# A decoder layer with attention, a state-space branch and 16 experts: three expert halves requested before the last projection job, decay products in bf16 parts, the router's logits in four streams, and two products of resident rows ahead of the ranks

## The reference

```python
sh1, sc1, gt1, sh2, sc2, gt2 = split(silu(c) @ w_mod + b_mod, 6)
h = rms_norm(x, g_norm1) * (1 + sc1) + sh1
q, k, v, fl, z, xbc, dtr, ga, gb = split_cols(h @ w_in)
o_att = forgetting_attention(rms_norm(q), rms_norm(k), v, cumsum(log_sigmoid(fl + b_f)))
u = silu(causal_conv(xbc)); xs, bm, cm = split_cols(u)
dt = softplus(dtr + dt_bias); acs = cumsum(dt * a)          # per chunk of 128 tokens
lmat = exp(acs[t] - acs[s])                                  # for s <= t, per head
y = (cm @ bm.T * lmat) @ (xs * dt) + (cm * exp(acs)) @ state + d_skip * xs
y = group_rms_norm(y * silu(z)) * g_ssm
x = x + gt1 * ((sigmoid(ga) * (o_att @ w_pa) + sigmoid(gb) * (y @ w_pb)) @ w_o)
h2 = rms_norm(x, g_norm2) * (1 + sc2) + sh2
probs = softmax(h2 @ w_router + b_router)    # 16 experts in 4 groups
# group with the largest probability, its two best experts, weights normalised over the two
x = x + gt2 * sum_over_two(w * ((silu(h2 @ w_gate[e]) * (h2 @ w_up[e])) @ w_down[e]))
```

## Time and profile before

| | |
|---|---|
| timed runs | 795.19, 796.26, 804.49 us; median 796.26 |
| profiled execution | 794.72 us, of it span 793.1 us |
| PE / weight loads / DVE / ACT / POOL busy | 757.5 / 523.0 / 366.0 / 296.7 / 94.4 us |
| chain that ended last | PE 75%, DVE 7%, ACT 6%, DMA 5%, issue 4% |
| DMA | 219.5 MB, mean 277 GB/s |
| mean granted clock of PE | 0.989 |

### The profile page before, as it was taken

How to read it: one execution, slowest core, us unless ns; L and a number is a source line. 1 busy time by engine, 2 the same in 40 slices (tenths; PEclk the granted TensorE clock), 3 DMA queues, 4 the chain that set the end, 5 groups by cost and what they waited for, 6 DMA issues and landing times.

```text
span 793.1 us, 12477 instructions
## 1 busy us (share of the span) xinstructions
PE 757.5 (96%) x4545; PEld 523.0 (66%) x4545; DVE 366.0 (46%) x852; ACT 296.7 (37%) x736; POOL 94.4 (12%) x155
## 2 busy tenths in 40 slices
PE   3799999999999999999998999999999999999997
PEld 3376787778785687888877888888444444444444
DVE  1355657777773186587999211022321223122214
ACT  3223257657773224668884001012412112221212
POOL 3321012112101114320100100000010000000000
PEclk9799999999999999999999999999899999999999
DMA  9996365969866512349999694363999999999992
GB/s 319 331 343 190 107 199 156 337 213 330 271 230 205 179 54 60 111 143 376 372 313 363 220 402 156 107 248 128 385 380 420 420 420 420 418 421 418 423 407 73
DMA packets 94040, 219.48 MB, mean 277 GB/s; under 512 B 11765, under 2 KB 67645, under 8 KB 80024
## 3 DMA queue, kind: packets, MB, share of 16 engines
q1 hardware_dynamic: 78928, 181.71, 62.7%
q0 software_dynamic: 7840, 31.67, 11.7%
q10 hardware_dynamic: 7208, 5.25, 2.1%
HBM read 207.05 MB, written 13.22 MB: 278 GB/s over the span
## 4 chain that ended last, share of the span: by engine, by line
PE 75%; DVE 7%; ACT 6%; DMA 5%; issue 4%; SPq 1%; POOLq 1%; ACTq 0%; POOL 0%; DVEq 0%
PE bank L1681 16%; PE bank L2015 14%; PE bank L1911 7%; PE bank L2039 7%; PE bank L1614 4%; PE bank L1919 4%; PE bank L2058 3%; PE bank L1893 3%; DMA conv_out<-in_w_mod 3%; PE bank L1677 2%; PE bank L1635 2%; DMA arena<-in_state_ssm 2%; DVE arena L1417 1%; ACT arena L1031 1%; PE bank L1828 1%
## 5 line engine op out<-in xcount | busy, mean ns | idle before, releaser
L1681 PE MATMUL bank<-h_normed,weight_ring 128*128 128x264 f32 x1024 | 237.2, 388 | 1.7 <-ACT conv_work L1039 1.7
L1681 PEld LDWEIGHTS bank<-h_normed,weight_ring 128*128 128x128 f32 x1024 | 191.4, 190 | 36.9 <-issue 3.5
L2015 PE MATMUL bank<-arena,h_normed 128*64 128x512 f32 x176 | 79.0, 604 | 0.0
L1911 PE MATMUL bank<-y_T,weight_ring 128*128 128x264 f32 x256 | 57.4, 386 | 0.4 <-DVE y_T L1454 0.4
L1541 DVE SCALAR_TENSOR_TENSOR x_residual<-bank,modulation,x_residual 128x256 f32<-128x256 f32 x64 | 28.8, 484 | 55.4 <-PE bank L2058 55.4
L1911 PEld LDWEIGHTS bank<-y_T,weight_ring 128*128 128x128 f32 x256 | 48.5, 190 | 8.7 <-issue 0.5
L1534 DVE TENSOR_TENSOR arena<-arena,bank 128x512 f32<-128x512 f32 x8 | 8.5, 1066 | 98.5 <-PE bank L2015 98.5
L1614 PE MATMUL bank<-identity,arena 128*128 128x128 f32 (+5 forms) x218 | 31.6, 287 | 13.6 <-ACT arena L859 9.6
L1031 ACT ACTIVATE arena<-conv_out,early_small 128x128 f32<-128x128 f32 x128 | 38.3, 388 | 11.3 <-DVE arena L1417 10.7
L2015 PE MATMUL bank<-weight_ring,h_normed 128*64 128x512 f32 x144 | 42.0, 594 | 0.0
L1614 PEld LDWEIGHTS bank<-identity,arena 128*128 128x128 f32 (+5 forms) x218 | 26.4, 152 | 22.5 <-POOL arena L713 9.6
(11 more groups left out here) (374 smaller groups left out, 1208.2 us busy)
## 6 DMA issues: line engine op xcount, KB each, us to landing
weight_ring<-in_w_in SPq DMA_DIRECT2D x36, 1024.0 KB, 6.3
weight_ring<-in_w_mod SPq DMA_DIRECT2D x22, 1024.0 KB, 10.0
arena<-in_w_up SPq DMA_DIRECT2D x12, 1024.0 KB, 20.0
weight_ring<-in_w_down SPq DMA_DIRECT2D x12, 1024.0 KB, 23.3
arena<-in_w_gate SPq DMA_DIRECT2D x10, 1024.0 KB, 17.7
weight_ring<-in_w_gate SPq DMA_DIRECT2D x10, 1024.0 KB, 14.8
arena<-in_state_ssm POOLq DMA_DIRECT2D x8, 1024.0 KB, 10.1
out_ssm_sample<-arena POOLq DMA_DIRECT2D x8, 1024.0 KB, 8.3
```

What stands on the lines that cost most here:

```text
L1681: ins = mm(ps[:, 0:T], w, hT[:, c, :], start=c == 0, stop=c == KD - 1)
L1911: ins = mm(ps[:, 0:T], w, yT[:, c, :], start=c == 0, stop=c == NXB - 1)
L2015: ins = mm(banks[i][BLK * e:BLK * e + BLK, :], xg[:, 4 * h + c, BLK * e:BLK * e + BLK], ws[e][c], start=h == 0 and c == 0, stop=h == 1 and ...
```

## The change

Five edits:

1. Early expert halves. Half 16 goes behind `pb` 7. The ring's slots are filled singly, each when its own last `o` job is done, in the order of these jobs. Ahead of the last ring part SP waits for the merged branches and loads half 15. Half 13 follows behind `o` 7. The last slot in the arena is moved by 128 columns for that.
2. Decay products. The running sums are split in three bf16 parts (rounded value, rounded rest, rest of that), stacked in 96 partitions by DVE and two transfers of ACT; `ab` multiplies them by a 96-row one-hot matrix `head_pick` in bf16. A pair is no longer interleaved over two row strips. The copy to partitions 64 up goes away.
3. The `exp` job goes. The skip vector comes by a fifth transfer on ACT, behind the three scratch stores (four requests), and DVE makes `dsk` from it by two copies behind a wait for all of them. The bank rotation is turned by one from `bt` on, so that all later jobs keep their banks.
4. Logits. `lg` is done for two blocks at a time, as four products of 264 columns on four column strips of 32: two for the logits of the two blocks (weights padded to 32 columns), two for the squares' sums. A job `lgt` follows: ACT copies the 264 columns to SBUF, PE folds the strips and turns them to rows by three products with a 0/1 matrix `fold`. Two of the six `hx` jobs go ahead: one ahead of the last `lg`, one ahead of the fold.
5. Ahead of the ranks, two products of 256 columns of `ones` with a block of x into the bank of the ranks, read by nobody. The weights' semaphore is merged in that of the assignment.

Core of the diff:

```diff
-        jobs += [("bs", 0), ("bs", 1), ("exp",)]
+        jobs += [("bs", 0), ("bs", 1)]
...
-            if i:
-                jobs += [("lg", i - 1)]
-        jobs += [("lg", 7)] + [("hx", a, f) for a in range(3) for f in range(2)] + [("rk",)]
+            if i and i % 2 == 0:
+                jobs += [("lg", i // 2 - 1)]
+        jobs += [("lg", 3), ("lgt",)] + [("hx", a, f) for a in range(3) for f in range(2)] + [("rk",)]
...
+        ring_places = sorted(((8 + 4 * (k // 2) + k % 2 + 2 * q, 2 * i + q) for k, i in enumerate(ring_order) for q in range(2)),
+                             key=lambda p: (jobs.index(last_user[held_by[p[1]]]), p[0]))
...
-            for i in ring_order:
-                filled_by(ring_last[i])
-                n = 4 + ring_order.index(i)
-                load_expert(n)
-            filled_by(("o", 7))
-            load_expert(7)
             load_half(16)
+            for m, i in ring_places:
+                if i == ring_places[-1][1]:
+                    sp.wait_ge(m_ready, KD)
+                    load_half(15)
+                filled_by(last_user[held_by[i]])
+                load_half(m)
+            load_half(13)
...
                         act.dma_start(se_d, ex[:]).then_inc(bs_out, 16)
+                        act.dma_start(dskf, t["d_skip"].to_broadcast([128, SH])).then_inc(bs_out, 16)
...
                     if a == 0 and b == 0:
-                        dve.wait_ge(bs_out, 64)
+                        dve.wait_ge(bs_out, 80)
+                        for q in range(2):
+                            r = slice(64 * q, 64 * q + 64)
+                            link(v.tensor_copy(dsk[r, :], dskf[r, q:SH:2]))
...
-                    for i in range(4):
-                        for q in range(2):
-                            h, r = 4 * (b + q) + i, 64 * q
-                            ins = mm(pair[q][:, 128 * i:128 * i + 128],
-                                     ident[r:r + SH, r + h:r + h + 1].to_broadcast([SH, 128]),
-                                     acsT[r:r + SH, 128 * a:128 * a + 128], start=True, stop=True)
+                    for q in range(2):
+                        for i in range(4):
+                            h = 4 * (b + q) + i
+                            ins = mm(pair[q][:, 128 * i:128 * i + 128], head_pick[:, h:h + 1].to_broadcast([3 * SH, 128]),
+                                     acs3[:, 128 * a:128 * a + 128], start=True, stop=True)
+                        done(ins, ("ab", a, b + q))
...
+                    for q in range(2):
+                        mm(sbank[32 * q:32 * q + 32, 0:T], wr32[:, 2 * r + q, :], hT[:, 2 * r + q, :], start=r == 0,
+                           stop=r == 3, tile_position=(0, 32 * q), skip_group_check=True)
+                    for q in range(2):
+                        ins = mm(sbank[64 + 32 * q:96 + 32 * q, 0:T], onesf[:, 0:32], sqr[:, (2 * r + q) % 4, :], start=r == 0,
+                                 stop=r == 3, tile_position=(0, 64 + 32 * q), skip_group_check=True)
...
+                elif k == "lgt":
+                    rows_flipped(("hx", 0, 1))
+                    pe.wait_ge(lgs_ready, 1)
+                    for a, (t0, n) in enumerate(TOK):
+                        ins = mm(logits[0:n, a, 0:NE + 1], lgs[:, t0:t0 + n], fold[:], start=True, stop=True)
+                    ins.then_inc(lgt_done, 1)
...
+                    for _ in range(2):
+                        mm(ps[:, 0:NP], onesf[:], xT[:, 0, 0:NP], start=True, stop=True)
```

More of the change, by code:

```diff
@@ L682, in _ @@
             link(g.memset(cT, 0.0), consts)
+            for p in range(3):
+                r = slice(SH * p, SH * p + SH)
+                link(g.tensor_copy(head_pick[r, :], ident[r, r]))
             link(g.memset(onesf[:], 1.0))
@@ L919, in _ @@
                     link(fn(fdw[0:SH, 2, 0:128], fdw[0:SH, 2, 0:128], ACT.Exp))
-                    link(fn(ex[:, NS:2 * NS], ex[:, NS:2 * NS], ACT.Exp), fd_e)
+                    link(fn(ex[:, NS:2 * NS], ex[:, NS:2 * NS], ACT.Exp), fd_exp)
                 elif k == "ft":
                     read_out(act, j)
+                    act.wait_ge(acs_split, 1)
+                    for p in range(2):
+                        act.dma_start(acs3[SH * (p + 1):SH * (p + 2), :], acs_low[:, NP * p:NP * p + NP])\
+                           .then_inc(acs_stacked, 16)
                     act.dma_start(t["logf_prompt"].rearrange("o b (a p) h -> p (o b a) h", p=128),
```

134 lines of the change are left out of this document (76 added, 58 removed).

## The result

| | before | changed |
|---|---|---|
| timed runs beside each other, 16 each: median (lowest to highest) | 797.05 (795.15 to 804.49) us | 794.29 (788.48 to 799.97) us |
| ratio changed / before | | 0.9943, interval 0.9918 to 0.9969 |
| profiled execution, span | 793.1 us | 798.0 us |
| mean granted clock in it | 0.989 | 0.973 |

The ratio is 4.5 us of gain (2.5 to 6.5). The forecast was a gain of 6.0 by the medians (796.26 to 790.3). The profiled execution of the changed kernel is the slowest of its 16, 4.9 us of span longer than the one of before, so its profile has to be read by stages, and not by its end.

The account below looks back on a forecast made before the run. PE sets the pace, with transfers near their limit in the expert stage. Logits 4.4 plus decay 1.9 minus 0.5 after the last `o` minus 0.4 for the skip vector gives 5.4 us off: timed median 790.3 us, range 785.5 to 796.

Parts of the forecast that it names:

- the prediction's own case: Whole kernel: the summed terms hold, timed median 790.3 us, range 788 to 793, chance 0.56.
- Logits: Between `o` jobs: three groups of four products replace six slots of small products, gain 4.4 us.
- After the last `o`: Last logit group to ranks: square root comes later, some of it regained, net cost 0.5 us (0.2 to 1.2).
- Decay products: `ab` pairs: bf16 products at 0.10 us each, 0.27 less a pair, seven pairs, gain 1.9 us (1.0 to 4.6).
- the rival that spoke of the floor: `ab` pairs: bf16 products near their floor, 0.44 us a pair, another 2.7 us off, 787.6; chance 0.12.
- Skip vector: Ahead of the first decay pair: removed products gain nothing, ACT's extra request costs 0.4 us (0.2 to 0.8).
- The 2 us bring nothing: First decay pair: without the 32 products PE arrives 2 us earlier but only waits for ACT's copies.
- Three halves: Expert weight stream: asking for three halves earlier is worth nothing in itself, since the stream breaks before the first freed half.
- the prediction's own sign of being wrong: Profile after: a clock of 0.5 anywhere in 277 to 285 or through the gather would show the prediction wrong.
- The rival with two more low stretches of 1.8 us on the path: New pauses ahead of first decay pair and ranks lower the clock: gain only 1.8 us, 793.9; chance 0.16.
- The stretch at the gate: First gate products: a rival had the low-clock stretch miss them, 1.8 us more gained, 788.5; chance 0.08.
- the rival that had 0.04: Gather and gate start: all at 1.2 GHz, 7 to 9 us lost, 798.3; chance 0.04.

Follow-up runs that it names:

- u_skip: Changed kernel with edit 3 undone (spreading products back, skip vector's transfer and two copies gone): 793.5 us, ratio 0.9924 to before.
- best: skip_early with the shift products ahead of the ranks replacing the resident products there, and resident products in two other PE waits: 792.24 us, ratio 0.9927 to before.
- best_state: best with eight more resident products in three PE waits of the state stage: 791.15 us, ratio 0.9906 to before.
- dense10: Changed kernel with ten products of resident rows instead of two, spread from the last logit group to the token numbers: 795.04 us, ratio 0.9954 to before.
- again: Changed kernel unaltered, timed and profiled once more: 795.69 us, ratio 0.9937 to before.
- u_decay: Changed kernel with edit 2 undone (float32 decay products on two row strips): 798.81 us, ratio 0.9997 to before.
- u_logits: Changed kernel with edit 4 undone (twelve small products of a block behind each projection job): 798.22 us, ratio 0.9995 to before.
- skip_early: Changed kernel with the skip vector's transfer moved to SP near 28 us and DVE's copies made earlier: 791.79 us, ratio 0.9906 to before.

## Why the forecast was right, and where it was not

The median, 794.29, is in the range of 785.5 to 796, but outside the 788 to 793 that the prediction's own case allowed, and 4.0 above the 790.3 forecast (0.8 of it is that before's median is 797.05 here and not 796.26). That the gain, 4.5 us, came near the 5.4 of the sum is in part luck: the parts are worth 3.1 more than forecast at full clock, and about 4.0 were lost in two ways, one that the sum left to the rivals and one that it didn't have.

**Logits: right.** 4.4 us were forecast, and the stage is 35.59 - 30.98 = 4.6 shorter in every profile that has the edit. The group costs 0.58, not 0.46; what made up for it is that `o` jobs back to back take 3.56 to 3.66, not 3.76.

**After the last `o`: right.** 0.5 forecast, 8.35 - 8.01 = 0.34 found; the square root 1.94 us behind the group where 2.1 stood.

**Decay products: mechanism right, size wrong.** The step that failed is the price of a bf16 product of 128 columns. It was taken as 0.10 us, from a 16-column row and a quarter of float32's price per column; it is 0.61 / 8 = 0.076 in the timeline, 0.55 / 8 = 0.069 in the chain, and 0.45 / 8 = 0.056 in the chain for two of the six pairs that counted. These six, not seven, gained 4.1 us, not 1.9: 0.54 to 0.64 in the pair itself, and 0.14 in the projections right behind four of them, which the prediction did not reckon with. That is nearer the rival that spoke of the floor (7 x 0.65 = 4.6) than the case chosen. The Trainium skill's figure for it, about 81 ns on the page "TensorE: Matmul & The Clock Gate", section "Back-to-back issue gap", would have given 3.1, nearer than the forecast.

**Skip vector: sum nearly right, both reasons wrong.** 0.4 us of cost forecast, 0.62 found (u_skip). "The 2 us bring nothing" was wrong: from the turning to the first pair it took 6.59 us with `exp` and float32, 5.88 now and 5.40 with the request gone too. ACT's copies begin 4.55 us after the turning, one request more ahead of them, where before had 5.12: the store to `sx_scratch` held ACT for 1.42 us before and 0.40 now. In both profiles with `exp` one of these requests was 1.0 us longer than in the twelve without it; why is not shown. The claim that DVE's longer wait for the new vector ends at about the same time as its wait for PE was wrong by 1.9 us, for the vector lands late and the copies meet POOL's multiply.

**Three halves: right.** No effect seen, and the stream breaks as described.

**Low clock: the prediction's own sign of being wrong was seen.** It named a clock of 0.5 through the gather. The rival with two more low stretches of 1.8 us on the path had 0.16 and gives 793.9; that the median is near this is no proof of it. A stretch behind the pause of the first decay pairs is in three profiles (73.56 or 73.57 us to the fourth store, for 71.88), at 1.7 us. With edit 4 and up to four resident products the gather and what surrounds it took 17.2 to 17.9 us from ranks to gate in eight of eleven profiled executions (best and best_state among them) and 13.7 to 14.1 in the other three; without edit 4, 12.1 and 12.4. The stretch at the gate went away in dense10 and best alone. So up to 5.5 us are lost between ranks and gate, by the mechanism of the rival that had 0.04, but together with a gain of 8.5 and not 5.4.

**Missed: ACT's fourth store request, and a stage behind it in which nothing is made up.** The prediction took each microsecond that PE wins ahead as a microsecond of the end. As far as the fourth store that held: again comes to it 3.0 us earlier than before (357.50 for 360.50). Then the request holds ACT for 3.88 us instead of 0.39, ACT's first state update begins at 361.50 (361.01 before), and the first `o` job at 515.08 (515.12 before): all 3.0 us are gone. From the first state update to the first `o` job it is 154.1 us before, and 153.6 in each of again, u_skip, u_decay, u_logits and dense10, which have no low clock on the way, though they begin it anywhere from 357.62 to 364.28. The chain there runs over ACT, DVE, PE and the transfers of the samples' states, DVE is busy 9.89 of the 10 us from 370 to 380, and about as much in the next three windows, before and now, and PE waits 3.8 us there before, 6.5 in again. So the stage passes its start on as it is, late or early: what took the gain back is the request, 0.39 to 4.17 us long.

Put together: at full clock and with a short request the edits are worth 0.1 + 4.1 + 4.6 - 0.3 = 8.5 us. The profiled execution gave it all back: 4.3 from the store to the first `o` (158.93 - 154.62; 3.6 the request's length, the rest low clock), 1.7 in the decay stage at low clock (73.57 - 71.88), 5.5 from ranks to gate and 0.7 behind. 8.5 - 4.3 - 1.7 - 5.5 - 0.7 is -3.7, and the later start of its first stages (273.24 for 271.99 at the turning) makes the 4.9 of the spans. Over many executions about 4.0 of the 8.5 are lost. How these split isn't settled: only profiled executions show the request, and before has one, with 0.39. At equal mean clock the gain is 5.4 us, so 3.1 of the 4.0 do not go with a lower mean clock (an estimate); they can be the request, or low stretches that lay over waits before and lie on the path now. Nor is it settled what makes the request long. It isn't the order of this change: skip_early had 4.17, best, with the same instructions there, 0.39.

## What to carry to other kernels

Before adding up what PE saves, ask what the next engine on the chain does with an earlier start: here ACT came 3.0 us earlier to a transfer request and was held by it for 3.5 us more, and the 60 us of DVE work behind it had no slack to make that up. Time taken out of TensorE's small products is real, but look where the stretches of half clock lie afterwards: before, one lay over work that waited anyway, and with edit 4 it lay over the gather in most profiles. And a transfer that replaces products must be asked for long before: the same edit cost 0.6 us in place and gained 1.8 early.

## What was new about the hardware

- Two DVE copies of 64 x 16 float32 values took 2.14 us while POOL multiplied 128 x 2048 values from SBUF, and 0.41 where POOL computed nothing. Beside it the first copy ended 0.03 us after the multiply. The Trainium skill's page "SBUF — State Buffer", section "SBUF: two separate sides", has the two engines share a pair of ports as an exclusive lock; the two rows agree.
- A bf16 product of 128 columns with 128-column weights from 96 rows took 0.056 to 0.069 us of the chain, in rows of eight.
- One transfer request of ACT took 0.39 to 4.17 us in 14 profiled executions of like programs, the three like it just ahead 0.39 to 0.42 in each.
- TensorE's clock stood at 1.2 GHz from 560 to 570, the gather products of 561.40 to 570 included, which kept it busy without a pause; ahead of that were 10 us of pauses, transposes and small products (549.1 to 559) during which it was still at 2.4. It did not fall in the one profile where ten full products stood among these pauses and small products, and did where four of them, or four and the two eight-row products, filled only the pauses.
